# The feed-forward down projection by Strassen's seven block products instead of 22 plain steps, in a one-core fp32 kernel of two transformer blocks

## The chip, the core and the metric

One core of a Trainium2 chip runs the whole program as one launch. The metric is the device time of that core in microseconds (us), taken over several runs; lower is better. The profile is of one execution.

## The reference

Two transformer blocks on a batch of one with 1024 tokens of width 1024, all in fp32: retention and pooling mixers, cross attention, a feed-forward layer, then a gated delta rule layer ("GDN") and a forgetting attention. The change touches only the last matrix product of the feed-forward layer of the first block. `D_FF` is 2816.

```python
def conv_glu_ffn(h, w_up, conv_w, conv_b, w_down):
    a = h @ w_up
    ...
    c = conv_w[0] * a2 + conv_w[1] * a1 + conv_w[2] * a + conv_b
    gate, val = jnp.split(c, 2, axis=-1)
    return (jax.nn.silu(gate) * val) @ w_down
...
        x = x + conv_glu_ffn(rmsnorm(x, ffn_norm_g[l]), ffn_w_up[l], ffn_conv_w[l],
                             ffn_conv_b[l], ffn_w_down[l])
    return rmsnorm(x, final_norm_g)
```

## The kernel before

Everything is kept transposed: a tile has 128 channels on the partitions and tokens along its length. Each fp32 operand is split into a high part, rounded to the matmul format (ScalarE or GpSimd makes it), and a low part, value minus high part (VectorE or GpSimd). One product of a 128 by 128 weight block with 128 by 512 activations is `dot3`: three matmuls of 128x512 (high by high, high by low, low by high, L1011 to L1013) into one half of a PSUM bank pair.

**Around the stage.** The up projection runs in 22 pairs (`PAIRS`), each already by seven block products (`PRODUCTS`), and leaves the gated activation of a pair, 128x1024, in DRAM (`act_store`, L686, from the buffer `taps`). After the last pair VectorE still folds the products together (L3028 to L3053), applies the taps of the convolution (L3062) and the gate (L3073, which counts `ff_prod`). After the down projection comes the final norm, whose sums run beside the first GDN gemm: `next_high` (L2290) and `lo_gained` (L3118) split the rows of x that are finished.

**The down projection.** 22 steps (`DOWN`), eleven for the first four of the eight 128-row tiles of the output and eleven for the last four. In a step TensorE multiplies the eight weight blocks of one 128x1024 slab with two 128x1024 activation tiles: 16 `dot3`, 48 matmuls, into four bank pairs (`DOWN_BANKS`). So 352 `dot3` in all, the plain count for 22 contraction tiles, 8 row tiles and 2 token halves.

**Who feeds it.** SP loads one 512 KB slab of weights a step (`down_load`, L670) and two activation tiles (`ring_load`, L681) into a ring of five buffers; GpSimd splits the slab (`split_slot`, L819 high and L828 low, 128x1024 each); ScalarE makes the high part of the activations (`ring_high_part`, L2238), VectorE the low part (`ring_low`, L3080). The activation tiles are loaded twice but for the last two, 20 times two tiles. At the end of each half VectorE adds the four bank pairs to x in SBUF (`down_add`, L3114, eight of 128x1024). Order on each engine is the program's own, written out by hand: an instruction waits with all that stands behind it. On VectorE `ring_low(0)` stands inside the last pair's work, ahead of L3033, and `ring_low(1)` behind L3053. On SP the eight loads that bring x back (L730) go between the slabs.

## Time and profile before

| | us |
|---|---|
| median of 3 runs | 2753.74 |
| lowest and highest | 2750.53, 2755.33 |
| span of the profiled execution | 2752.7 |
| TensorE busy | 2696.4 (98%) |
| VectorE, ScalarE, GpSimd busy | 1451.5, 1068.8, 1127.4 |
| down projection, first matmul to the first one of the GDN layer | 1117.32 to 1363.83 |

The profile puts a time of start and a duration to each instruction of the four engines and to each DMA. A row of a timeline may join several equal instructions in a row ("x6"); its duration is then from the first one's start to the last one's end. A matmul's record, 0.39 to 0.40 us, overlaps the next one's: the distance of the starts is what counts. Idle time in front of an instruction stands in brackets, with what ended it. The mean granted clock of TensorE in the stage is 1.00.

### The profile page before, as it was taken

Reading aid. Unit: us, or ns where it says so; the run is one execution under the profiler, and the core shown is the slowest. Engines: PE = TensorE matmul, PEld = TensorE weight load, DVE = VectorE, ACT = ScalarE, POOL = GpSimd, SP = SyncE. Lnnn points to the kernel's source line nnn. Section 1 sums busy time; section 2 is a strip of 40 time slices with the busy share of each in tenths; the row PEclk is TensorE's granted clock in tenths of the full one; section 3 lists DMA queues with packets and bytes.
Section 4 is the critical chain, followed back from the end, with each engine's and each line's share of the span. In section 5 each row is a group of like instructions: output and inputs, shape, how many; then the busy total and the mean of one; then the engine's idle time right before and its main releaser. Section 6 shows DMA issues by size and latency. Waiting matters only on the chain.

```text
span 2752.7 us, 34759 instructions
## 1 busy us (share of the span) xinstructions
PE 2696.4 (98%) x13662; PEld 2197.4 (80%) x13662; DVE 1451.5 (53%) x2038; ACT 1068.8 (39%) x1614; POOL 1127.4 (41%) x625
## 2 busy tenths in 40 slices
PE   8999999999999999999999999999998999999998
PEld 6888788777788888788878888888876888888886
DVE  7344643136666666522356666666535455555565
ACT  5322222234444444222244554544534433333342
POOL 4333443224777776433322122222345333333335
PEclk9999999999999999999999999999998999999999
DMA  4112231003222222554322222222222111111114
GB/s 152 31 40 75 101 106 54 25 30 114 71 77 84 77 84 77 192 174 139 122 74 68 67 72 65 70 65 66 65 100 85 39 39 39 39 39 39 39 54 164
DMA packets 111787, 214.24 MB, mean 78 GB/s; under 512 B 32032, under 2 KB 61888, under 8 KB 111504
## 3 DMA queue, kind: packets, MB, share of 16 engines
q1 hardware_dynamic: 104992, 190.02, 21.2%
q10 hardware_dynamic: 6192, 20.18, 2.0%
q8 instruction: 109, 1.79, 0.3%
q0 software_dynamic: 448, 1.88, 0.2%
q14 instruction: 46, 0.38, 0.0%
HBM read 177.38 MB, written 34.67 MB: 77 GB/s over the span
## 4 chain that ended last, share of the span: by engine, by line
PE 88%; DVE 5%; ACT 2%; issue 2%; DMA 1%; POOL 1%; SPq 0%; ACTq 0%; DVEq 0%; POOLq 0%
PE gemm L1011 21%; PE gemm L1012 20%; PE gemm L1013 20%; PE small L1193 2%; PE small L1736 2%; PE small L1013 2%; PE small L1012 2%; PE small L1011 2%; PE small L1724 1%; PE small L1581 1%; PE gemm L1134 1%; PE small L1306 1%; PE small L1326 1%; PE gemm L1137 1%; PE gemm L1138 1%
## 5 line engine op out<-in xcount | busy, mean ns | idle before, releaser
L1011 PE MATMUL gemm<-h_hi,w_hi 128*128 128x512 f32 x2136 | 894.6, 419 | 22.7 <-DVE h_lo L2722 8.9
L1012 PE MATMUL gemm<-h_lo,w_hi 128*128 128x512 f32 x2136 | 845.1, 396 | 0.0
L1013 PE MATMUL gemm<-h_hi,w_lo 128*128 128x512 f32 x1960 | 776.6, 396 | 0.0
L819 POOL TENSOR_TENSOR w_hi<-w_raw,unit_col 128x1024 fp32r<-128x1024 f32 x134 | 262.6, 1960 | 1134.4 <-PE gemm L1013 891.6
L1011 PEld LDWEIGHTS gemm<-h_hi,w_hi 128*128 128x128 f32 x2136 | 403.9, 189 | 106.5 <-issue 11.2
L1012 PEld LDWEIGHTS gemm<-h_lo,w_hi 128*128 128x128 f32 x2136 | 404.3, 189 | 74.8 <-issue 2.9
L1013 PEld LDWEIGHTS gemm<-h_hi,w_lo 128*128 128x128 f32 x1960 | 369.3, 188 | 89.6
L828 POOL TENSOR_TENSOR w_lo<-w_raw,w_hi 128x1024 fp32r<-128x1024 f32 x118 | 305.3, 2587 | 13.8 <-DVE w_lo L2881 4.9
L972 POOL TENSOR_TENSOR w_hi<-w_raw,unit_col 128x1024 fp32r<-128x1024 f32 x32 | 60.8, 1899 | 310.9 <-PE gemm L1013 310.9
L3080 DVE TENSOR_TENSOR t_lo<-t_lo_f,t_hi 128x1024 fp32r<-128x1024 f32 x36 | 44.5, 1282 | 143.1 <-ACT t_hi L2238 143.1
L2541 ACT ACTIVATE xres<-xres,stat 128x128 f32<-128x128 f32 (+3 forms) x64 | 49.7, 777 | 151.0 <-DVE stat L3553 150.7
L3062 DVE SCALAR_TENSOR_TENSOR small<-norm,vec,small 128x1024 f32<-128x1024 f32 x84 | 106.0, 1285 | 1.5
L3547 DVE SCALAR_TENSOR_TENSOR xres<-small,rstd_cols,xres 128x128 f32<-128x128 f32 x64 | 22.4, 350 | 155.9 <-PE small L1013 155.4
L1011 PE MATMUL gemm<-t_hi,w_hi 128*128 128x512 f32 x248 | 98.2, 396 | 0.0
L1012 PE MATMUL gemm<-t_lo,w_hi 128*128 128x512 f32 x248 | 98.1, 396 | 0.0
L2238 ACT ACTIVATE t_hi<-t_lo_f 128x1024 fp32r<-128x1024 f32 x36 | 35.9, 1050 | 156.7 <-DMA t_lo_f<-act_spill 156.7
L2635 ACT ACTIVATE xres<-small 128x512 f32<-128x512 f32 (+2 forms) x96 | 47.1, 491 | 105.5 <-PE small L1724 104.9
L1013 PE MATMUL gemm<-t_hi,w_lo 128*128 128x512 f32 x204 | 80.6, 395 | 0.0
L1736 PEld LDWEIGHTS small<-xres 128*128 128x128 f32 x576 | 74.1, 191 | 5.7
L974 POOL TENSOR_TENSOR w_lo<-w_raw,w_hi 128x1024 fp32r<-128x1024 f32 x32 | 76.8, 2399 | 2.5
L1736 PE MATMUL small<-xres 128*128 128x128 f32 x576 | 74.5, 274 | 0.0
L964 POOL TENSOR_TENSOR w_raw<-w_raw,vec 128x1024 f32<-128x1024 f32 x32 | 66.5, 2078 | 1.8 <-DMA w_raw<-w_stream 1.8
(550 smaller groups left out, 5258.1 us busy)
## 6 DMA issues: line engine op xcount, KB each, us to landing
w_raw<-w_stream SPq DMA_DIRECT2D x178, 512.0 KB, 3.5
t_lo_f<-act_spill SPq DMA_DIRECT2D x36, 512.0 KB, 4.4
act_spill<-taps SPq DMA_DIRECT2D x22, 512.0 KB, 2.9
x_spill<-xres ACTq DMA_DIRECT2D x16, 512.0 KB, 2.7
v_gate<-w_stream SPq DMA_DIRECT2D x11, 512.0 KB, 4.2
v_val<-w_stream SPq DMA_DIRECT2D x11, 512.0 KB, 3.4
xres<-x_t SPq DMA_DIRECT2D x8, 512.0 KB, 8.7
xres<-x_t ACTq DMA_DIRECT2D x8, 512.0 KB, 4.9
```

The costliest lines, as they stand in the source:

```text
L819: nc.gpsimd.tensor_tensor(whi[d][:, :, :], raw[s][:, :, :], unit, ALU.mult).then_inc(w_hi_done, 1)
L828: nc.gpsimd.tensor_tensor(wlo[d][:, :, :], raw[s][:, :, :], whi[d][:, :, :].bitcast(F32), ALU.subtract).then_inc(w_split, 1)
L964: nc.gpsimd.tensor_tensor(raw[s][:, :, :], raw[s][:, :, :], gain.broadcast_to([P, KT, P]), ALU.mult).then_inc(w_gained, 1)
L972: nc.gpsimd.tensor_tensor(whi[s][:, :, :], raw[s][:, :, :], unit, ALU.mult).then_inc(w_hi_done, 1)
L974: nc.gpsimd.tensor_tensor(wlo[s][:, :, :], raw[s][:, :, :], whi[s][:, :, :].bitcast(F32), ALU.subtract).then_inc(w_split, 1)
L1011: mm(dst, w_hi, a_hi, start=first, stop=False, skip_group_check=onto)
L1012: mm(dst, w_hi, a_lo, start=False, stop=False, skip_group_check=onto)
L1013: return mm(dst, w_lo, a_hi, start=False, stop=last, skip_group_check=onto)
L1193: last = nc.tensor.transpose(ck(dst, n), ck(src, n), ident)
L1736: last = mm(ck(pb, 4 + q % 4), ck(X4(0), b), ck(X4(5), b), start=(b == 0), stop=(b == q))
L2541: A(sc, sc, ACT.Exp, bias=stat[:, 14 + z:15 + z], accum_out=stat[:, 15 + z:16 + z]).then_inc(fx_exp, 1)
L3062: ins = V.scalar_tensor_tensor(c, Nf[:, v * FP + n:v * FP + n + S], vc("ff_w", 2 * PAIRS * n + q), c, ALU.mult, ALU.add)
```

## The change

The contraction (22 tiles) is cut in two halves of eleven, the output rows in two halves of four tiles and the tokens in two halves of 512: a 2 by 2 by 2 block product, computed as Strassen's seven. Each product is eleven **units** (one contraction tile each) of four `dot3`, 308 in all, from sums or differences of weight blocks and of activation blocks. They run in four groups: two products beside each other, three times (`part` 0 in `A_BANKS`, `part` 1 in `B_BANKS`, the latter one unit behind), then one product alone. n counts units over the groups, so unit 11 is the first of group 1 (the groups are numbered 0 to 3). The operations of one unit, all 128x512 or 128x4x128:

| group | GpSimd: sums L1136, low L1153 | ScalarE highs | VectorE: sums L3364, lows L3369, L3375, late L3380, L3385 | `dot3` |
|---|---|---|---|---|
| 0 | 1, 1 | 4 | 4 | 8 |
| 1 | 2, 1 | 4 | 5 | 8 |
| 2 | 1, 1 | 4, 5 from u = 3 | 4 (u = 0, 1), 5 (u = 2), 6 from u = 3 | 8 |
| 3 | 1, 0 | 1 | 1, and `lo_gained` | 4 |

The split weights and the split sums lie in buffers three deep: what is prepared for unit n waits until unit n - 3 has been multiplied (`unit_mm` at n - 2). "Late" operations prepare in group 2, from u = 2, the activation sums of group 3. In a unit of groups 0 to 2 the order on GpSimd is sum(s), wait for ScalarE's high part, low. When a product ends, its four banks of 128x512 are added to one or two of the four quarters of x: 48 additions (L3401) of 128x512; the next group may not write a bank until they are done.

Activations stay in SBUF as halves of tokens (`B11`, `B21`, `B12`, `B22`, eleven strips each, in the buffers of `h_hi_f`, `h_lo_f`, `yt` and `head`) and are loaded once, up to five strips a DMA (`act_load`, L840). Weight slabs are loaded 52 times (`raw_load`, L835) into six buffers, then four others. On SP slabs 4 and 5 of that list stand behind the last `act_store`.

```diff
-DOWN = [(0, i) for i in range(FF_STEPS)] + [(1, FF_STEPS - 1), (1, FF_STEPS - 2)] + [(1, i) for i in range(FF_STEPS - 2)]
...
+SLABS = (((0, 1), (1, 1)), ((0, 0), (1, 1), (0, 1)), ((0, 0), (1, 0)), ((1, 0), (1, 1)))
+N_RAW, N_LATE = 6, 4
...
+        TARGETS = {(0, 0): ((C21, ALU.add), (C22, ALU.subtract)), (0, 1): ((C11, ALU.add), (C21, ALU.add)),
+                   (1, 0): ((C11, ALU.add), (C22, ALU.add)), (1, 1): ((C22, ALU.add),),
+                   (2, 0): ((C12, ALU.add), (C22, ALU.add)), (2, 1): ((C11, ALU.subtract), (C12, ALU.add)),
+                   (3, 0): ((C11, ALU.add),)}
...
+        A_BANKS = [b[:, c * HALF:(c + 1) * HALF] for b in (ps[0], gp[1]) for c in range(2)]
+        B_BANKS = [b[:, c * HALF:(c + 1) * HALF] for b in (ps[1], gp[0]) for c in range(2)]
...
+            act_load(R2, (0, 4), (SECOND[0], 0), b21_in[0])
+            raw_load(3)
             act_store(PAIRS - 1)
...
+            act_load(R2, (4, 8), (SECOND[4], 0), b21_in[1])
+            for j in (4, 5, 6, 7):
+                raw_load(j)
...
+                if g == 0:
+                    down_sum(n, (0, 1), (1, 1), (0, 1), ALU.add)
+                elif g == 1:
+                    down_sum(n, (0, 0), (1, 1), (1, 1), ALU.add)
+                    down_sum(n, (0, 1), (0, 0), (0, 1), ALU.subtract)
...
+                pool.wait_ge(*w_rounded(2 * n + 1))
+                nc.gpsimd.tensor_tensor(dw_low(n, 0), dw_value(n, 0), dw_hi(n, 0).bitcast(F32), ALU.subtract).then_inc(w_a_ready.sem, 1)
...
+            for g in range(GROUPS):
+                for u in range(UNITS):
+                    unit_products(UNITS * g + u, 0)
+                    if u and g < GROUPS - 1:
+                        unit_products(UNITS * g + u - 1, 1)
+                if g < GROUPS - 1:
+                    unit_products(UNITS * g + UNITS - 1, 1)
...
                 if p == PAIRS - 1:
-                    ring_low(0)
+                    down_t_low(0, 0)
...
                 if p == PAIRS - 1:
-                    ring_low(1)
+                    down_w_low(0)
+                    down_t_low(1, 0)
+                    down_t_sum(0, 1)
+                    down_w_low(1)
+                    down_t_low(0, 1)
                 tap(p, 0, 1)
                 tap(p, 0, 0)
+                if p == PAIRS - 1:
+                    down_t_sum(1, 1)
+                    down_w_low(2)
+                    down_t_low(2, 0)
                 tap(p, 1, 1)
+                if p == PAIRS - 1:
+                    down_t_low(1, 1)
                 tap(p, 1, 0)
                 product(p)
...
+                for part in range(2):
+                    if g and u == part:
+                        for q in range(4):
+                            bank_add(g - 1, part, q)
```

**The end of the up projection.** On VectorE, in the kernel before, from the last pair's work with gemm1 to the gate (lines as in the profile):

```order
L3080 TENSOR_TENSOR h_lo<-h_lo_f,h_hi 128x1024 x2
L3033 TENSOR_TENSOR tiny<-gemm1,tiny 128x512
L3035 TENSOR_TENSOR gemm1<-gemm1,poolw 128x512
L3041 TENSOR_TENSOR gemm0<-gemm0,tiny 128x512
L3043 TENSOR_TENSOR norm<-gemm0,norm 128x512
L3049 TENSOR_TENSOR gemm1<-gemm1,tiny 128x512
L3051 TENSOR_TENSOR gemm1<-gemm1,tiny 128x512
L3053 TENSOR_TENSOR norm<-gemm1,norm 128x1024
L3080 TENSOR_TENSOR h_lo<-h_lo_f,h_hi 128x1024 x2
L3062 SCALAR_TENSOR_TENSOR taps<-norm,vec,taps 128x1024 x4
L3073 TENSOR_TENSOR taps<-taps 128x1024
```

The same place in the changed kernel, first the head and then what stands from its L3322 (L3053 before) to the gate:

```order
L3369 TENSOR_TENSOR h_lo<-h_hi_f,h_lo 128x512
L3302 TENSOR_TENSOR tiny<-gemm1,tiny 128x512
```

```order
L3322 TENSOR_TENSOR norm<-gemm1,norm 128x1024
L3375 TENSOR_TENSOR w_lo1<-w_raw1,w_lo1 128x512
L3369 TENSOR_TENSOR h_lo<-h_hi_f,h_lo 128x512
L3364 TENSOR_TENSOR h_lo_f<-yt,h_hi_f 128x512
L3375 TENSOR_TENSOR w_hi1<-w_raw1,w_hi1 128x512
L3369 TENSOR_TENSOR h_lo<-h_lo_f,h_lo 128x512
L3331 SCALAR_TENSOR_TENSOR taps<-norm,vec,taps 128x1024 x2
L3364 TENSOR_TENSOR h_lo_f<-yt,h_hi_f 128x512
L3375 TENSOR_TENSOR norm_r<-tiny,norm_r 128x512
L3369 TENSOR_TENSOR h_lo<-h_hi_f,h_lo 128x512
L3331 SCALAR_TENSOR_TENSOR taps<-norm,vec,taps 128x1024
L3369 TENSOR_TENSOR h_lo<-h_lo_f,h_lo 128x512
```

Two operations of 128x1024 ahead of L3033 have become one of 128x512; the two ahead of the taps have become nine of 128x512, spread between them.

**Group 1.** On GpSimd, the operations of unit 11; in the kernel before a step had the two of the second fence:

```order
L1136 TENSOR_TENSOR w_raw0<-norm,w_raw0 128x4x128
L1136 TENSOR_TENSOR w_raw1<-w_raw1,norm 128x4x128
L1153 TENSOR_TENSOR w_ex<-w_raw0,w_ex 128x512
```

```order
L819 TENSOR_TENSOR w_hi<-w_raw,unit_col 128x1024
L828 TENSOR_TENSOR w_lo<-w_raw,w_hi 128x1024
```

On VectorE, one unit in the midst of group 1, where the kernel before had two operations of 128x1024 a step:

```order
L3364 TENSOR_TENSOR h_lo_f<-h_hi_f,head 128x512
L3364 TENSOR_TENSOR h_lo_f<-h_hi_f,h_lo_f 128x512
L3369 TENSOR_TENSOR h_lo<-h_lo_f,h_lo 128x512 x2
L3375 TENSOR_TENSOR w_hi1<-w_raw1,w_hi1 128x512
```

None of the five has an operand in PSUM. The additions out of the banks stand between two units; here those of group 1's first product, at the start of group 2:

```order
L3375 TENSOR_TENSOR w_hi1<-norm,w_hi1 128x512
L3401 TENSOR_TENSOR xres<-xres,small0 128x512 x4
L3401 TENSOR_TENSOR xres<-xres,gemm1 128x512 x4
L3364 TENSOR_TENSOR h_lo_f<-h_hi_f,yt 128x512
L3369 TENSOR_TENSOR h_lo<-h_lo_f,h_lo 128x512
L3369 TENSOR_TENSOR h_lo<-yt,h_lo 128x512
L3375 TENSOR_TENSOR norm_r<-norm,norm_r 128x512
```

Eight additions of 128x512 stand ahead of all activation sums and lows of the next unit. The same stage end in the kernel before had one addition of 128x1024 for each bank pair and nothing to prepare behind it but a step that was due later.

## Rows read from the trace of the kernel before

**Rows 1.** The page: span; busy time of the engines; the chain by engine.

```profile
span 2752.7 us, 34759 instructions
...
PE 2696.4 (98%) x13662; PEld 2197.4 (80%) x13662; DVE 1451.5 (53%) x2038; ACT 1068.8 (39%) x1614; POOL 1127.4 (41%) x625
...
PE 88%; DVE 5%; ACT 2%; issue 2%; DMA 1%; POOL 1%; SPq 0%; ACTq 0%; DVEq 0%; POOLq 0%
```

**Rows 2.** Busy time by stretch: the down projection.

```profile
core 0: us, PE busy (x) PEld busy (x) DVE busy (x) ACT busy (x) POOL busy (x), PEclk, DMA share, GB/s
1117.20:1363.80 246.60, 246.60 (x1058) 197.98 (x1057) 76.16 (x62) 51.38 (x51) 95.03 (x44) 1.00 0.44 152
```

**Rows 3.** Timeline of PE: the last product of the up projection, and both ends.

```profile
start us, us, engine line op out<-in xcount [idle before <-releaser]
1112.34 0.40 PE L1013 MATMUL gemm<-t_hi,sum_ex_r 128*128 128x512 f32 x1
1114.47 0.47 PE L1011 MATMUL gemm<-t_hi,pair_ex 128*128 128x512 f32 x1 [1.74 <-DVE tiny L3033]
...
1117.32 0.39 PE L1011 MATMUL gemm<-h_hi,w_hi 128*128 128x512 f32 x1
```

```profile
1363.83 0.39 PE L1011 MATMUL gemm<-h_hi,w_hi 128*128 128x512 f32 x1
```

**Rows 4.** Timeline of DVE across the start of the stage.

```profile
1109.67 4.06 DVE L3080 TENSOR_TENSOR h_lo<-h_lo_f,h_hi 128x1024 fp32r<-128x1024 f32 x2 [4.25 <-ACT h_hi L2238]
1113.65 0.68 DVE L3033 TENSOR_TENSOR tiny<-gemm,tiny 128x512 f32<-128x512 f32 x1
...
1117.52 0.70 DVE L3049 TENSOR_TENSOR gemm<-gemm,tiny 128x512 f32<-128x512 f32 x1 [0.49 <-PE gemm L1013]
1118.12 0.69 DVE L3051 TENSOR_TENSOR gemm<-gemm,tiny 128x512 f32<-128x512 f32 x1
1118.85 1.23 DVE L3053 TENSOR_TENSOR norm<-gemm,norm 128x1024 f32<-128x1024 f32 x1
1119.99 2.54 DVE L3080 TENSOR_TENSOR h_lo<-h_lo_f,h_hi 128x1024 fp32r<-128x1024 f32 x2
...
1127.60 1.22 DVE L3073 TENSOR_TENSOR taps<-taps 128x1024 f32<-128x1024 f32 x1
```

**Rows 5.** The line L2967, VectorE, min/median/max ns; and DVE at its last four.

```profile
L2967 DVE TENSOR_TENSOR t_lo<-t_lo_f,t_hi x12: 681/684/1775, 644.5 to 692.5; 128x512 fp32r<-128x512 f32 x12
```

```profile
688.48 5.75 DVE L2967 TENSOR_TENSOR t_lo<-t_lo_f,t_hi 128x512 fp32r<-128x512 f32 x4
```

**Rows 6.** Timeline of POOL: one alone, and three beside those four.

```profile
661.91 1.30 POOL L927 TENSOR_TENSOR w_raw<-w_raw 128x512 f32<-128x512 f32 x1
...
690.39 1.61 POOL L927 TENSOR_TENSOR v_val<-v_val 128x512 f32<-128x512 f32 x1
692.08 1.60 POOL L936 TENSOR_TENSOR sum_ex<-v_val,v_gate 128x512 f32<-128x512 f32 x1
693.75 1.62 POOL L908 TENSOR_TENSOR v_gate_r<-v_gate,w_hi 128x512 fp32r<-128x512 f32 x1
```

**Rows 7.** Timelines of DVE and POOL at the end: an operand in PSUM, and none.

```profile
1364.03 1.22 DVE L3114 TENSOR_TENSOR xres<-small,xres 128x1024 f32<-128x1024 f32 x1 [0.39 <-PE small L1013]
1365.17 1.88 DVE L3118 SCALAR_TENSOR_TENSOR h_lo<-xres,both_g,h_hi 128x1024 fp32r<-128x1024 f32 x1
```

```profile
1364.07 1.90 POOL L819 TENSOR_TENSOR w_hi<-w_raw,unit_col 128x1024 fp32r<-128x1024 f32 x1 [6.74 <-PE small L1013]
```

**Rows 8.** Timeline of ACT: a high part of 128x512.

```profile
1084.79 0.63 ACT L2125 ACTIVATE w_hi<-v_gate 128x512 fp32r<-128x512 f32 x1 [1.25 <-PE gemm L1013]
```

**Rows 9.** Landing time of a slab (page), and two stretches with their DMA rate.

```profile
w_raw<-w_stream SPq DMA_DIRECT2D x178, 512.0 KB, 3.5
```

```profile
1100.00:1120.00 20.00, 18.26 (x79) 14.33 (x77) 14.45 (x15) 7.43 (x9) 9.83 (x4) 1.00 0.77 254
1120.00:1124.00 4.00, 4.00 (x19) 3.14 (x18) 3.96 (x5) 1.24 (x1) 0.31 (x1) 1.00 1.02 401
```

More of the change, by code:

```diff
@@ new lines, in build, with raw_view @@
+        W_TWO = ((whi[0][:, :, :], wlo[1][:, :, :]), (wlo[0][:, :, :], whi[1][:, :, :]), (w_ex[:, :, :], tile8(N_r[:, 3, :])))
+        W_LATE = [tile8(hlo[:, k, :]) for k in (4, 5, 6)]
+        RAWS = [raw[0][:, :, :], raw[1][:, :, :], tile8(const[:, CONST_AT["dmat"]:CONST_AT["dmat"] + S]),
+                tile8(tiny[:, :, :].rearrange("p i x -> p (i x)")),
+                tile8(N[:, 0, :]), tile8(N[:, 1, :])] + [tile8(hhi_f[:, k, :]) for k in range(4, KT)]
+        def raw_view(n, half, row):
+            return RAWS[raw_of(raw_for(n, half, row))].rearrange("p (q k) m -> p k q m", k=2)[:, odd_of(n, half)]
@@ new lines, in dt_low, with dt_value, summed @@
+        def dt_low(n, part):
+            return T_LO[n % 3][part] if n < N_TWO else B21_r[n % UNITS]
+        def dt_value(n, part):
+            g, u = divmod(n, UNITS)
+            if (g, part) == (0, 0):
+                return B11[u]
+            if (g, part) == (2, 1):
+                return B22[u]
+            return T_SUM[n % 3][part]
+        def summed(g, part):
+            return (g, part) not in ((0, 0), (2, 1))
+        C11, C12, C21, C22 = (KT // 2, 0), (KT // 2, 1), (0, 0), (0, 1)
@@ new lines, in t_sums, with w_sums, bank_count @@
+        def t_sums(n, part):
+            return sum(summed(m // UNITS, at) for m, at in ORDER[:t_place(n, part)])
+        def w_sums(n, part):
+            g, u = divmod(n, UNITS)
+            return sum(W_SUMS[:g]) * UNITS + W_SUMS[g] * u + (1 + part if g == 1 else 1)
+        def bank_count(g, part, q):
+            done = 0
+            for key in TARGETS:
+                each = 1 if key == (2, 0) else len(TARGETS[key])
+                if key == (g, part):
+                    return done + each * (q + 1)
+                done += 4 * each
@@ new lines, in _ @@
+            act_load(R2, (10, 11), (SECOND[10], 0), b21_in[1])
+            for k in range(KT):
+                if k == KT // 2:
+                    for j in (8, 9):
+                        raw_load(j)
+                sp.dma_start(xres[:, k, :], x_keep[k]).then_inc(x_back.sem, 16)
+            raw_load(10)
+            act_load(R2, (UNITS, 2 * KT), (SECOND[0], 1), b22_in)
+            act_load(R1, (UNITS, 2 * KT), (FIRST[0], 1), b12_in)
+            for j in (11, 12, 13):
+                raw_load(j)
@@ L733, in g_row @@
+            act_load(R2_H, (0, 5), (SECOND[CUT], 1), b22_in)
+            act_load(R2_H, (5, 6), (SECOND[UNITS - 1], 1), b22_in)
+            act_load(R1_lo, (0, UNITS - CUT), (FIRST[CUT], 1), b12_in)
+            for j in range(14, len(RAW_LOADS)):
+                raw_load(j)
             def g_row(h):
@@ L2277, in _ @@
                     high_a22(p + 1)
+            down_t_high(0, 1)
             tap2(PAIRS - 1, 1)
+            down_w_high(2, 0)
+            down_t_high(2, 0)
+            down_w_high(2, 1)
+            down_t_high(1, 1)
             gate(PAIRS - 1)
-            for j in range(2, FF_STEPS + 1):
-                ring_high_part(j)
+            for n in range(3, N_TWO):
+                g, u = divmod(n, UNITS)
+                if u == 0:
+                    down_t_high(n - 1, 1)
+                down_w_high(n, 0)
+                down_t_high(n, 0)
+                down_w_high(n, 1)
+                if u:
+                    down_t_high(n - 1, 1)
+                if g == GROUPS - 2 and u >= 3:
+                    down_late_high(u - 3)
+            down_t_high(N_TWO - 1, 1)
+            for u in range(UNITS - 3, UNITS):
+                down_late_high(u)
             def next_high(k):
```

444 lines of the change are left out of this document (312 added, 132 removed).

## The prediction, made before the run

> **What bounds the kernel now.** I read the page first: TensorE is busy 98% of the span and makes 88% of the chain that ends last [rows 1]. Then the table by stretches for the down projection: 246.6 us, TensorE busy for all of them at a granted clock of 1.00, while VectorE works 76, ScalarE 51 and GpSimd 95 us there, and the DMA moves 152 GB/s [rows 2]. So in this stage TensorE is the bound, the others have room, and work taken from it is worth its full time until another engine is full. From the first matmul to the first of the next layer [rows 3] it is 1363.83 - 1117.32 = 246.51 us for 352 `dot3`: 0.70 us each. All other questions are whether VectorE, GpSimd, ScalarE and the DMA can feed a TensorE that needs less.
>
> **TensorE's own gain.** 308 `dot3` in place of 352: 44 x 0.70 = **-30.8 us**. It all lies on the path.
>
> **The last pair of the up projection.** TensorE stalls 1.74 us for L3033, which waited on VectorE behind two ring lows that took 4.06 us [rows 3, 4]. Now one operation of 128x512 stands there, at most 1.78 us [rows 5], so L3033 is done early enough that TensorE goes on at 1112.34 + 0.23 = 1112.57 in place of 1114.47: **-1.9 us**, and the stage may start at 1115.4.
>
> **What one operation costs on VectorE and GpSimd.** This is the step the rest hangs on. A VectorE operation of 128x512 takes 0.68 us alone and starts 0.60 after the last one [rows 4, 5], and one of GpSimd 1.30 [rows 6]. But the slowest of L2967's twelve took 1.775 us, and four in a row took 5.75 us, just where GpSimd's operations went from 1.30 to 1.61 each and started 1.69 apart [rows 5, 6]: the two engines take turns, one operation of each in 1.69 us. VectorE loses 1.69 - 0.60 = 1.09 us at each such meeting. It is not so where VectorE reads PSUM: L3114 kept its 1.22 us under a GpSimd operation that covers it, while L3118 right after it, with no PSUM operand, took 1.88 [rows 7]. All preparation of the new stage is without PSUM operands; the 48 additions have one and cost 0.60 each, undisturbed. I take GpSimd's 128x4x128 sums at the 1.30 of 128x512, as the nearest row with two plain operands; bounds are 1.27, no gain from the form, and 1.6, the value under contention.
>
> The Trainium skill (SBUF — State Buffer, section "SBUF: two separate sides") calls this port an exclusive lock: whoever starts first keeps it for the whole instruction and the other fully blocks. By it a meeting would cost VectorE the full 1.30, 0.21 more than the rows' 1.09, and the sum would be larger by 0.21 x (3 x 11 + 2 x 8) = 10 us. The rows decide for turns of 1.69. The same section confines the lock to VectorE operations with two SBUF inputs; by that rule, the trace agrees for L3114.
>
> **Start of the stage: +9.4 us.** If TensorE never waited, unit 4 would start after seven blocks of 4 x 0.70 = 2.8 us: 1115.4 + 19.6 = 1135.0. Its weights are slabs 4 and 5, which SP issues only once `ff_prod` is complete. That was 1127.60 + 1.22 = 1128.8 [rows 4]. Now: 1.9 earlier; less 2.5 for the ring lows that went; plus nine operations of 0.60, 5.4; plus two or three meetings of 1.09, for units 1 to 3 are being prepared on GpSimd meanwhile, 2.5: about 1132.4. Behind it SP issues 0.5 MB of the store, 1 MB of activations and then the two slabs, 1 MB. At some 400 GB/s [rows 9] 2.6 MB take 6.6 us, and a lone slab of 0.5 MB takes 3.5, 2.2 more than its 1.3 of transfer [rows 9]: landed at 1141. Then sum 1.3, high 0.63 [rows 8], low 1.3: TensorE at 1144.4. Smaller waits before it (the bank of L3322 at 1118.1, the lows of units 1, 2 and 3 behind taps) are inside these 9.4. Bounds: 7.4, with no meeting before `ff_prod`; 12, with all transfers at 254 GB/s [rows 9] and partly hidden.
>
> **Group 0, otherwise: 0.** Four VectorE and two GpSimd operations a unit: 2 x 1.69 + 2 x 0.60 = 4.6 us, against 8 x 0.70 = 5.6 of TensorE, which hides them. ScalarE's four take 2.5.
>
> **Group 1: +15.5 us.** Five VectorE operations and three meetings: 5 x 0.60 + 3 x 1.09 = 6.27, and 0.24 for handing over between the engines: 6.51 us a unit. TensorE's 5.6 no longer cover it: 0.91 x 11 = 10.0. At the boundary the 16 additions of group 0 (9.6 us) stand ahead of the next units' sums; buffers three deep give back some of it; 5.5 stay. Bounds: 3.3, all of it the boundary, with no meetings; 19, with GpSimd at 1.6 for the sums.
>
> **Group 2: +17.0 us.** From u = 3 on six VectorE operations, two meetings, and a gap of 1.3 us while the two late operations and the lows wait for ScalarE in order: 3.6 + 2.2 + 1.3 = 7.1 us against 5.6: 1.5 x 8 = 12.0, with 0.8 before; boundary with 12 additions (group 1's) 4.2. Bounds: 6, if VectorE fills its gaps (2 x 1.69 + 4 x 0.60 = 5.8 a unit); 19.
>
> **Into group 3: +4.1 us.** Unit 33's weights need ScalarE and VectorE behind the last late lows, and its banks the eight additions of the product before: some four us between 4 and 6. Inside group 3 a unit needs one operation of each engine in 2.8 us: nothing.
>
> **End: +1.5 us.** Three `lo_gained` now come together with the last four additions, and the chain of the final norm that followed L3118 starts later by a bit more than one operation of 1.2 us. Bounds 0 and 3.
>
> **Sum.** -30.8 - 1.9 + 9.4 + 15.5 + 17.0 + 4.1 + 1.5 = +14.8 us. The profiled execution's span is 2752.7, 1.0 below the median of the runs, so 2767.5 of span, **2768 us** of time: TensorE gives up 31 us of work and gets 46 of waiting.
>
> **Rival A: TensorE stays the bound (faster).** If sums and lows of VectorE and GpSimd meet seldom, because GpSimd runs ahead of VectorE by a unit and they fall in each other's gaps, VectorE needs 3.6 us a unit at most and group 1 waits 3.3, group 2 0.9, the start 7.4, the last boundary 4.2: 15.8. Then -32.7 + 15.8 + 1.5 = -15.4: 2738 us. For it: stages in which both engines are half busy and TensorE runs on. Against: in group 1 GpSimd works 3.9 of 5.6 us, and rows 5 and 6 show every operation met. It decides from a cost of a meeting under 0.5 us: then group 1 needs 3.0 + 1.5 + 0.2 = 4.7.
>
> **Rival B: the meetings are there but fall into idle time (no change).** VectorE's loop is then its bare capacity: group 1 6.27, so 0.67 x 11 = 7.4 and 3.3 at the boundary; group 2 5.8, so 1.4 and 4.2; start 9.4; last boundary 4.1: 29.8. Net -1.4: 2752 us. For it: the gap of 1.3 in group 2 is worked out from an order of waits that no row shows. Against: in-order waits rarely close up by themselves.
>
> **Rival C: the DMA (slower still).** Between 1134 and 1180 some 18 MB must come (slabs 6 to 14, x, the rest of the activations), 393 GB/s. The stretch of 1120 to 1124 gave 401, the 20 us around it 254 [rows 9]. At 254 it is 71 us in place of 46; 5.5 of the 25 would hide in group 1's boundary: +19.5, 2788 us. The Trainium skill (DMA: Bandwidth & Descriptors, section "Specifications") names 358 GB/s as a core's share of HBM; by that estimate it would be 50 us, and +4; the trace shows 401, above it.
>
> **Rival D: the change does not do what it says.** The count of matmuls is in the instruction order, 924 for 1056; nothing there could fail unseen. No chance of its own.
>
> **Chances.** Forecast 0.60 (2756 to 2779, from the bounds of its terms: start -2 to +2.6, group 1 -6 to +3.5, group 2 -8 to +2, taken as not all going one way); rival A 0.12; rival B 0.17; rival C 0.11. The range that holds 8 in 10 takes in the forecast's and B's and most of C's: 2749 to 2789. A measurement of this kernel tells 0.2%, 5.5 us, from no change. Faster by more: A and a bit of B, 0.13. Within: the most of B and the forecast's lowest edge, 0.17. Slower: 0.70.
>
> **What would show it.** In the profile of the changed kernel: TensorE's unit in group 1 every 6.5 us, with idle ended by VectorE's t_low or w_low (L3369, L3375) and these at 1.7 us where GpSimd's L1136 and L1153 run; a unit in group 2 every 7.1; unit 4 released by GpSimd behind a slab that landed near 1141; TensorE's first GDN matmul 13 us after 1363.8. Rival A shows units of 5.6 us; B 6.3 and 5.8; C idle ended by L1136 behind a DMA in group 0 or at unit 11. I am wrong if meetings are rare, or if the late operations of group 2 do not hold the sums of the next unit.

## The result and the profile after

| | before | after |
|---|---|---|
| median of 4 runs each, us | 2754.53 | 2779.45 |
| lowest, highest | 2750.53, 2758.9 | 2778.07, 2781.06 |
| span of the profiled execution | 2752.7 | 2777.4 |
| start of the down projection | 1117.32 | 1114.37 |
| first matmul of the next layer | 1363.83 | 1379.58 |

The ratio is 1.0087, with a 95% interval of 1.0073 to 1.0101: slower, by 24.9 us. TensorE has 30.8 us less to do and the program takes 25 us longer.

The page of the changed kernel, its span, busy times and chain by engine, as [rows 1] of before:

```profile
span 2777.4 us, 35061 instructions
...
PE 2682.0 (97%) x13530; PEld 2178.7 (78%) x13530; DVE 1602.0 (58%) x2214; ACT 1114.0 (40%) x1728; POOL 1161.5 (42%) x669
...
PE 82%; DVE 9%; issue 3%; ACT 3%; DMA 2%; POOL 1%; SPq 0%; ACTq 0%; DVEq 0%; POOLq 0%
```

The chain of waits now goes through VectorE for 9% of the span where it was 5% [rows 1]. Busy time by stretch (columns as in [rows 2]): the whole stage, the 10 us before the last gate, and the 6 us behind the longest stall.

```profile
1114.30:1379.60 265.30, 227.46 (x926) 173.87 (x926) 225.56 (x238) 95.79 (x162) 132.82 (x88) 0.97 0.42 154
1145.00:1151.00 6.00, 3.92 (x9) 3.15 (x10) 5.41 (x5) 3.33 (x8) 5.15 (x4) 0.50 1.04 408
1123.00:1133.00 10.00, 6.57 (x24) 4.96 (x23) 9.96 (x8) 4.51 (x8) 4.43 (x3) 0.83 0.00 1
```

In [rows 2] TensorE was busy for all of 246.6 us and VectorE for 76; here TensorE stands still for 38 of 265 and VectorE is busy for 226. The mean granted clock of the stage is 0.97, and in the second stretch 0.50, that is 1.2 GHz: this the prediction had in no term. TensorE's busy time falls by 14 us and not by 31, in part because a matmul at half clock counts as busy for longer.

The difference of the two traces, place by place. "Idle" is the distance of two starts less 0.233 us, summed over the gaps of a place (a place's units are those that the prediction's term counted); "half clock" is what matmuls 0.43 us apart cost over 0.233.

| place | forecast | measured |
|---|---|---|
| program before the last pair (unchanged) | 0 | -1.0 |
| last pair of the up projection | -1.9 | -2.0 |
| 308 products for 352 | -30.8 | -30.9 |
| start of the stage, to unit 5 | +9.4 | +11.6 idle, +3.3 half clock |
| group 1 | +15.5 | +11.6 |
| group 2, with its last unit | +17.0 | +15.5 idle, +1.5 half clock |
| into and in group 3 | +4.1 | +4.8 |
| small gaps | 0 | +1.4 |
| end: from the first product of the next layer to its small gates | +1.5 | +8.1 |
| behind it | 0 | +0.8 |
| sum | +14.8 | +24.7 |

### The profile page after: what moved, and what is told of

It reads as the page before. It is cut to its first block, busy times and chain, and to the rows that moved or that the text cites. A ratio compares the mean times of both kernels' runs of the same rounds, so it can differ in the third digit from the quotient of the medians.

```text
span 2777.4 us, 35061 instructions
## 1 busy us (share of the span) xinstructions
PE 2682.0 (97%) x13530; PEld 2178.7 (78%) x13530; DVE 1602.0 (58%) x2214; ACT 1114.0 (40%) x1728; POOL 1161.5 (42%) x669
## 3 DMA queue, kind: packets, MB, share of 16 engines
q8 instruction: 108, 1.77, 0.3%
q0 software_dynamic: 448, 1.88, 0.2%
## 4 chain that ended last, share of the span: by engine, by line
PE 82%; DVE 9%; issue 3%; ACT 3%; DMA 2%; POOL 1%; SPq 0%; ACTq 0%; DVEq 0%; POOLq 0%
PE gemm L1213 20%; PE gemm L1214 19%; PE gemm L1215 19%; PE small L1953 2%; PE small L1395 2%; PE small L1941 1%; DVE h_lo_f L3364 1%; PE small L1796 1%; PE gemm L1336 1%; PE gemm L1339 1%; PE gemm L1340 1%; PE small L1508 1%; PE small L1528 1%; PE small L1213 1%; DVE xres L3401 1%
## 5 line engine op out<-in xcount | busy, mean ns | idle before, releaser
L1214 PE MATMUL gemm<-h_lo,w_hi 128*128 128x512 f32 x2164 | 857.0, 396 | 0.0
L996 POOL TENSOR_TENSOR w_hi<-w_raw,unit_col 128x1024 fp32r<-128x1024 f32 x112 | 220.0, 1965 | 983.9 <-PE gemm L1215 885.4
L1005 POOL TENSOR_TENSOR w_lo<-w_raw,w_hi 128x1024 fp32r<-128x1024 f32 x96 | 250.0, 2604 | 12.1 <-DVE w_lo L3150 4.9
L1174 POOL TENSOR_TENSOR w_hi<-w_raw,unit_col 128x1024 fp32r<-128x1024 f32 x32 | 60.6, 1895 | 311.2 <-PE gemm L1215 311.2
L1953 PEld LDWEIGHTS small<-xres 128*128 128x128 f32 x576 | 74.1, 191 | 5.6
L1176 POOL TENSOR_TENSOR w_lo<-w_raw,w_hi 128x1024 fp32r<-128x1024 f32 x32 | 76.8, 2399 | 2.5
L3202 DVE TENSOR_REDUCE stat<-small 128x4 f32<-128x1024 f32 x8 | 9.8, 1225 | 106.2 <-PE small L1508 106.2
L3302 DVE TENSOR_TENSOR tiny<-gemm,tiny 128x512 f32<-128x512 f32 x22 | 15.2, 691 | 91.8 <-PE gemm L1215 91.8
L2718 ACT ACTIVATE v_new<-small,gdn_cols 128x128 f32<-128x128 f32 x64 | 23.5, 367 | 108.6 <-PE small L1721 108.6
L2441 ACT ACTIVATE small<-norm,vec 128x1024 f32<-128x1024 f32 x42 | 50.8, 1210 | 36.4 <-DVE norm L3312 20.5
L2481 ACT ACTIVATE h_lo<-h_lo_f 128x512 fp32r<-128x512 f32 x37 | 23.3, 629 | 101.8 <-DVE h_lo_f L3364 101.8
```

The costliest lines, as they stand in the source:

```text
L996: nc.gpsimd.tensor_tensor(whi[d][:, :, :], raw[s][:, :, :], unit, ALU.mult).then_inc(w_hi_done, 1)
L1005: nc.gpsimd.tensor_tensor(wlo[d][:, :, :], raw[s][:, :, :], whi[d][:, :, :].bitcast(F32), ALU.subtract).then_inc(w_split, 1)
L1174: nc.gpsimd.tensor_tensor(whi[s][:, :, :], raw[s][:, :, :], unit, ALU.mult).then_inc(w_hi_done, 1)
L1176: nc.gpsimd.tensor_tensor(wlo[s][:, :, :], raw[s][:, :, :], whi[s][:, :, :].bitcast(F32), ALU.subtract).then_inc(w_split, 1)
L1214: mm(dst, w_hi, a_lo, start=False, stop=False, skip_group_check=onto)
L1953: last = mm(ck(pb, 4 + q % 4), ck(X4(0), b), ck(X4(5), b), start=(b == 0), stop=(b == q))
```

## The experiments

Single executions on other chips differ by a few microseconds, so the experiments are compared by the stage's length (first matmul of the down projection to the first of the next layer; 265.2 us after, 246.5 before) and by what lies in it; a ratio is given where several rounds were run. The two runs of experiment 5 that leave the stage as it is have 263.1 and 263.6 us, so a difference of 2 us in a single execution says nothing. "Group" is the time from a group's first matmul to the next group's.

**1. Do VectorE and GpSimd take turns?** The midst of group 1 in the changed kernel, TensorE, VectorE and GpSimd:

```profile
1218.26 0.47 PE L1213 MATMUL small<-h_lo,w_hi 128*128 128x512 f32 x1 [0.71 <-DVE h_lo L3369]
1224.76 0.47 PE L1213 MATMUL small<-h_lo,w_lo 128*128 128x512 f32 x1 [0.75 <-DVE h_lo L3369]
1231.28 0.47 PE L1213 MATMUL small<-h_lo,w_ex 128*128 128x512 f32 x1 [0.70 <-DVE h_lo L3369]
```

```profile
1225.31 1.80 DVE L3375 TENSOR_TENSOR w_hi<-w_raw,w_hi 128x512 fp32r<-128x512 f32 x1
1227.04 1.77 DVE L3364 TENSOR_TENSOR h_lo_f<-h_hi_f,head 128x512 f32<-128x512 f32 x1
1228.74 1.79 DVE L3364 TENSOR_TENSOR h_lo_f<-h_hi_f,h_lo_f 128x512 f32<-128x512 f32 x1
1230.45 1.47 DVE L3369 TENSOR_TENSOR h_lo<-h_lo_f,h_lo 128x512 fp32r<-128x512 f32 x2
```

```profile
1225.27 1.30 POOL L1153 TENSOR_TENSOR w_ex<-tiny,w_ex 128x512 fp32r<-128x512 f32 x1 [1.81 <-ACT w_ex L2466]
1226.53 1.74 POOL L1136 TENSOR_TENSOR tiny<-const,tiny 128x512 f32<-128x512 f32 x1
1228.23 1.75 POOL L1136 TENSOR_TENSOR norm<-norm,const 128x512 f32<-128x512 f32 x1
```

A unit takes 6.50 and 6.52 us, released by VectorE's low. Of five VectorE operations the three that stand beside one of GpSimd's take 1.77 to 1.80, the other two 0.7 each; VectorE waits 0.1 us in a unit. That is the prediction's loop; the two runs that follow ask whether GpSimd is its cause.

The first takes one meeting away. It leaves out the second of GpSimd's two sums, and the group's second product takes the unsummed blocks:

```diff
                 elif g == 1:
-                    down_sum(n, (0, 0), (1, 1), (1, 1), ALU.add)
-                    down_sum(n, (0, 1), (0, 0), (0, 1), ALU.subtract)
+                    nc.gpsimd.tensor_tensor(raw_view(n, 1, 1), raw_view(n, 0, 0), raw_view(n, 1, 1), ALU.add).then_inc(w_summed.sem, 2)
```

> The changed kernel, with the second of the two weight sums that GpSimd makes in a unit of group 1 left out (the second product of that group takes the unsummed blocks; no other wait or transfer changes). Theory (VectorE and GpSimd take turns; each meeting costs VectorE 1.09 us): VectorE's five operations meet two instead of three, 5 x 0.60 + 2 x 1.09 + 0.24 = 5.4 us, under TensorE's 5.53, so a unit in the midst of group 1 falls from 6.5 to 5.5 us and group 1 loses about 7 us of waiting. Rival (VectorE is held by its own five operations and by waits for ScalarE, GpSimd costs nothing): a unit stays at 6.5 us.

Group 1 fell from 74.1 to 66.7 us, its idle time from 11.6 to 4.3, all of the rest at its boundary. Between 1217 and 1250 TensorE does not wait at all. VectorE's own operations are the same, and it hardly waited for ScalarE before or after (0.1 us a unit), so the rival falls.

The second adds two meetings where there was no wait:

```diff
                 if g == 0:
                     down_sum(n, (0, 1), (1, 1), (0, 1), ALU.add)
+                    if n >= 5:
+                        pool.wait_ge(*w_a_ready(n))
+                        for i in range(2):
+                            nc.gpsimd.tensor_tensor(tile8(N[:, 2, :])[:, 4 * i:4 * i + 4, :], raw_view(n, 1, 1), raw_view(n, 1, 1), ALU.add)
```

> The changed kernel, with two GpSimd additions of 128x512 more in each unit of group 0 from the sixth on; they write into a row that nobody reads, and stand in front of GpSimd's wait for ScalarE. Theory (turns): VectorE's four operations all meet one, 4 x 1.69 = 6.8 us, so these units go from 5.53 to 6.8 to 7.0 us, some 7 us more in all. Rival (GpSimd costs nothing by itself): its four operations take 5.2 us alone, less than 5.53, and the units stay.

VectorE and TensorE in that run:

```profile
1168.28 1.52 DVE L3379 TENSOR_TENSOR w_hi<-w_raw,w_hi 128x512 fp32r<-128x512 f32 x1
1169.72 1.52 DVE L3368 TENSOR_TENSOR h_lo_f<-yt,h_hi_f 128x512 f32<-128x512 f32 x1
1171.17 1.78 DVE L3373 TENSOR_TENSOR h_lo<-h_hi_f,h_lo 128x512 fp32r<-128x512 f32 x1
1172.87 1.77 DVE L3373 TENSOR_TENSOR h_lo<-h_lo_f,h_lo 128x512 fp32r<-128x512 f32 x1
```

```profile
1173.09 0.47 PE L1217 MATMUL small<-h_lo,w_ex 128*128 128x512 f32 x1 [0.16 <-DVE h_lo L3373]
1179.39 0.47 PE L1217 MATMUL small<-h_lo,w_hi 128*128 128x512 f32 x1 [0.51 <-DVE h_lo L3373]
1185.67 0.48 PE L1217 MATMUL small<-h_lo,w_lo 128*128 128x512 f32 x1 [0.53 <-DVE h_lo L3373]
```

All four VectorE operations are long now, and two units go from 5.53 to 6.30 and 6.28 us (of the six with added operations the first two stayed at 5.5, the third took 5.9 and the last 5.7); group 0 went from 76.3 to 80.7. The direction is as the theory says, the size below its 6.8: the two added operations read one operand twice, and a meeting with such a one takes 1.45 us (1168.28 to 1169.72), not 1.70, so that a unit of two such meetings and two full ones is 6.3 us.

**2. All of it to VectorE.** If GpSimd's help costs VectorE 1.1 us an operation and doing it itself costs 0.60, VectorE should do it alone. The edit moves sums and the first low from GpSimd's loop into VectorE's from the third unit on, and places the late operations as in the first edit of experiment 3 ("the run before" in its expectation):

```diff
+            def down_w_sum(n, i=0):
...
+                V.tensor_tensor(raw_view(n, *left), raw_view(n, *left), raw_view(n, *right), op).then_inc(w_summed.sem, 1)
...
             for n in range(3, N_TWO):
+                down_w_sum(n)
                 down_t_sum(n, 0)
+                if g == 1:
+                    down_w_sum(n, 1)
                 down_t_sum(n - 1, 1)
...
+                down_w_low_a(n)
                 down_t_low(n, 0)
                 down_w_low(n)
```

> The changed kernel, with GpSimd's work of the stage from the third unit on (weight sums and the first weight low, two or three operations a unit, one in group 3) given to VectorE, and the late operations placed as in the run before. GpSimd is then idle in the stage. Theory (turns): VectorE has eight operations a unit at 0.60 = 4.8 us with nobody to meet, under TensorE's 5.53: units of groups 1 and 2 at 5.5 us, only the boundaries and the start remain; about 2762 us against 2779. Rival (VectorE is full by its count of operations; a unit of group 1 shows 1.3 us an operation): eight would take 10 us a unit, 2860 us or more.

The same 45 us of group 1, first the changed kernel and then this run (columns as in [rows 2]):

```profile
1210.00:1255.00 45.00, 39.72 (x166) 30.35 (x165) 44.24 (x37) 16.66 (x30) 29.15 (x20) 1.00 0.30 109
```

```profile
1210.00:1255.00 45.00, 45.00 (x196) 36.56 (x195) 40.62 (x67) 19.68 (x33) 0.00 (x0) 1.00 0.41 152
```

VectorE does 67 instructions in less busy time (40.6 us) than 37 before (44.2), and TensorE never stops. 2768.95 us, ratio to the kernel before 1.0048 (1.0030 to 1.0065). The seven microseconds that were missing to 2762 have their own causes: units of group 2 took 6.57 us and not 5.5, with a wait of VectorE for ScalarE of 1.66 us in each (next experiment), and group 3, where VectorE's sums now stood in order behind slabs that landed late (waits of 1.4 to 5.2 us for them), went from 33.1 to 44.5 us.

**3. The late operations of group 2.** In the changed kernel VectorE and ScalarE there:

```profile
1296.84 0.69 DVE L3369 TENSOR_TENSOR h_lo<-h_lo_f,h_lo 128x512 fp32r<-128x512 f32 x1 [0.70 <-ACT h_lo L2481]
1297.88 0.69 DVE L3369 TENSOR_TENSOR head_r<-yt,head_r 128x512 fp32r<-128x512 f32 x1 [0.35 <-ACT head_r L2481]
```

```profile
1303.21 0.63 ACT L2481 ACTIVATE h_lo<-h_lo_f 128x512 fp32r<-128x512 f32 x1 [4.32 <-DVE h_lo_f L3364]
```

VectorE waits 1.05 us a unit for a ScalarE that has itself stood idle for 4.3: the sum, the high and the low of one operand stand too close together. The first edit put the late sum and low between them:

```diff
+                if g == GROUPS - 2 and u >= 2:
+                    down_late_sum(u - 2)
+                if g == GROUPS - 2 and u >= 3:
+                    down_late_low(u - 3)
                 down_t_low(n, 0)
...
                 down_w_low(n)
-                if g == GROUPS - 2 and u >= 2:
-                    down_late_sum(u - 2)
-                if g == GROUPS - 2 and u >= 3:
-                    down_late_low(u - 3)
```

> The changed kernel, with VectorE's late sum and late low of group 2 put between the activation sum and the first low of the unit, in place of behind the weight low. Same operations. Theory: 1.05 us of each unit of group 2 are waits of VectorE for ScalarE (0.70 before the first low, 0.35 before the second); the two late operations fill them, a unit falls from 7.04 to about 6.0 us, and group 2 by 7 to 9 us. Rival (the capacity of the pair VectorE and GpSimd is used up): a unit stays at 7.0.

The stage stayed at 264.0 us and group 2 at 79.3 (81.7 in the changed kernel, 80.1 in the two runs that leave it as it is). Single units ran unevenly, between 5.5 and 9.1 us; the seven from the third on took 6.9 on average. The expected gain did not come, yet this is not the rival's verdict, for the idle time was still there, elsewhere. VectorE in that run:

```profile
1298.96 0.69 DVE L3385 TENSOR_TENSOR yt_r<-yt,yt_r 128x512 fp32r<-128x512 f32 x1 [1.66 <-ACT yt_r L2486]
```

The late low waits for its high, and ScalarE works that off last, behind the high of the very sum that VectorE has just made. The second edit also moves it on ScalarE:

```diff
+                if g == GROUPS - 2 and u >= 3:
+                    down_late_high(u - 3)
                 down_w_high(n, 0)
...
-                if g == GROUPS - 2 and u >= 3:
-                    down_late_high(u - 3)
```

> As the run with the late operations between sum and lows, and ScalarE's late high put in front of the other highs of its unit, so that VectorE's late low finds it ready. Theory (in that run VectorE waited 1.66 us for ScalarE, in order behind the high of the unit's sum): no waits are left, 6 x 0.60 + 2 x 1.09 + 0.2 = 6.0 us a unit in group 2 against 7.04, 8 us less in all. Rival (capacity): 7.0 stays.

A unit takes 5.82 us, group 2 72.2 in place of 81.7 and the stage 255.9. Between 1290 and 1320 VectorE does not wait at all there: its six operations with their meetings fill the 5.8 us, and the other 1.2 us a unit of the changed kernel were an order.

**4. The start.** SP's slabs 4 and 5 landed at 1143.1; the row of GpSimd behind them, and TensorE's behind that:

```profile
1143.11 1.26 POOL L1136 TENSOR_TENSOR norm<-norm 128x512 f32<-128x512 f32 x1 [14.19 <-DMA norm<-w_stream]
```

```profile
1127.87 0.76 PE L1213 MATMUL small<-h_lo,w_ex 128*128 128x512 f32 x1 [3.43 <-DVE h_lo L3369]
...
1147.08 0.77 PE L1213 MATMUL small<-h_lo,w_lo 128*128 128x512 f32 x1 [6.41 <-DVE h_lo L3369]
1147.64 0.63 PE L1214 MATMUL small<-h_lo,w_lo 128*128 128x512 f32 x1
1148.07 0.63 PE L1215 MATMUL small<-h_lo,w_lo 128*128 128x512 f32 x1
```

The DMA had been idle from 1123 to 1133 (share 0.00 in the table above): everything stood behind the gate. The edit gives the two slabs another place, two rows of x that are free by then, and moves SP's issues ahead of the store:

```diff
+        XROWS = [tile8(xres[:, k, :]) for k in (1, 2)]
...
                 elif j in (4, 5):
-                    sp.wait_ge(ff_prod, PAIRS)
+                    sp.wait_ge(*prod_mm(PRODUCTS * PAIRS))
...
+            act_load(R2, (4, 8), (SECOND[4], 0), b11_in[0])
+            for j in (4, 5):
+                raw_load(j)
             raw_load(3)
             act_store(PAIRS - 1)
-            act_load(R2, (4, 8), (SECOND[4], 0), b21_in[1])
```

> The changed kernel, with the first use of slabs 4 and 5 moved from two rows of norm, which the taps still read, to two rows of x that are free once the last product of the up projection is done; SP issues them, and strips 4 to 7 of B21, ahead of the store of the last gated activation, and VectorE waits for those strips alone. Theory (the long stall before unit 4 is the way from the gate over the store to those slabs): the stall of 6.6 us before unit 4 falls to about 1, and since TensorE no longer stands still that long, its nine matmuls at half clock behind the stall (2.0 us) go too: 6 to 8 us less. Rival (VectorE's taps, gate and preparation alone hold unit 4): the stall shrinks by less than 3 us.

There is no gap before unit 4 any more; the stage is 258.2 us, 7.0 less, with 4.1 us idle left before unit 2, whose low stands on VectorE behind two taps and a wait of 1.2 us for ScalarE.

**5. The end, and the clock.** The prediction gave 1.5 us to the end; the trace shows 8.1. VectorE's three splits of x, met by GpSimd's first weight splits, and TensorE behind them:

```profile
1380.39 5.98 DVE L3434 SCALAR_TENSOR_TENSOR h_lo<-xres,both_g,h_hi 128x1024 fp32r<-128x1024 f32 x3
...
1381.77 3.40 DVE L3434 SCALAR_TENSOR_TENSOR h_lo<-xres,both_g,h_hi 128x1024 fp32r<-128x1024 f32 x1
...
1386.29 0.68 DVE L3485 COPY head<-small 128x512 f32<-128x512 f32 x1
```

```profile
1380.85 3.23 POOL L1005 TENSOR_TENSOR w_lo<-w_raw,w_hi 128x1024 fp32r<-128x1024 f32 x1
```

```profile
1397.66 6.99 PE L1686 MATMUL small<-const,head 128*128 128x1 f32 x32 [3.77 <-DVE head L3490]
```

Only the middle split (3.40 us, in the first row as one of the three) was held up for long; the others took 1.46 and 1.27. With them VectorE's chain for the norm starts 6.7 us after the first product of the next layer, where it started 3.1 after it before: that is TensorE's 3.6 us of new idle time. The other 4.5 of the 8.1 lie behind it: from the first of the 32 narrow matmuls to the small gates it is 14.1 us here and 9.6 before. The narrow ones took 3.73 us in the kernel before and 6.99 here, and 12 products behind them ran 0.43 us apart. Before, seven products did so too, at a granted clock of 0.50 with no more than 0.2 us idle in front of the narrow matmuls (columns as in [rows 2]):

```profile
1382.60:1385.60 3.00, 3.00 (x9) 2.32 (x8) 0.72 (x5) 0.30 (x1) 0.00 (x0) 0.50 0.51 144
```

The first run fills TensorE's idle time and changes nothing else:

```diff
                 if s == 9:
+                    pe.wait_ge(down_ev, KT)
+                    for _ in range(16):
+                        mm(gp[1][:, half(0)], whi[0][:, 0, :], hhi[:, 0, half(0)], start=True, stop=True)
                     pe.wait_ge(sq_added, SQ_FIN + 2 * KT)
```

> The changed kernel, with 16 matmuls of 128x512 more, into a bank whose contents have been added and that the next tile overwrites, in the 3.8 us in which TensorE stands still before L1686 at the end of the stage. Theory (part of the loss at the end is TensorE's clock, which falls after the idle time): with the gap filled L1686's 32 narrow matmuls take 3.7 us as before the change, not 7.0, and the products behind them run at 0.233 and not 0.43 us apart: 4 to 5 us less from the last addition to the small gates' product. Rival (the slow stretch has another cause, VectorE or the weights): no gain, or the cost of the filler.

```profile
1392.01 3.90 PE L1685 MATMUL gemm<-h_hi,w_hi 128*128 128x512 f32 x16
1395.87 5.09 PE L1689 MATMUL small<-const,head 128*128 128x1 f32 x32
```

L1686 (L1689 there) took 5.09 us, and the way from L1686 to the small gates 11.2 in place of 14.1: 2.9 us less, though VectorE was not touched. In five other runs with this end unchanged the same way took 12.6 to 13.8 and the narrow matmuls 6.5 to 7.0, so 1.4 to 2.9 us are what the stall costs through the clock. The expected 3.7 was not reached: from the twentieth on the narrow matmuls were slow even behind busy time.

The second run removes the cause, the order on VectorE:

```diff
-            for k in range(KT // 2, KT - 1):
-                lo_gained(k)
+            lo_gained(KT // 2)
             for i in range(2 * (KT - SUM_PE)):
...
-                if i == 3:
-                    lo_gained(KT - 1)
+            for k in range(KT // 2 + 1, KT):
+                lo_gained(k)
+            dve.wait_ge(h_lo_done, KT * HGDN + KT)
```

> The changed kernel, with only the first of the last three splits of x (lo_gained) ahead of the sums of the final norm on VectorE, and the others behind them. Theory (TensorE waits before L1686 for VectorE's sums, which stand behind three splits of 2.0 us each): the sums start 3 to 4 us earlier, the idle time before L1686 goes, and with it part of the slow clock behind it: 5 to 7 us less from the first product of the next layer to the small gates' product. Rival (ScalarE's squares hold the sums): under 2 us.

```profile
1392.03 3.63 PE L1686 MATMUL small<-const,head 128*128 128x1 f32 x32
```

No idle time, 3.63 us, and 22.1 us from the first product of the next layer to its small gates, where the changed kernel has 32.2 and the kernel before 24.1: 10 us less, more than the 5 to 7 expected. Not all of it is the order's: TensorE's clock stayed at 1.00 through this end, where the kernel before had its stretch at 0.50. Two later runs with the same order took 23.6 us, 8.6 less.

**6. Do the losses add up?** The three repairs of order of 3, 4 and 5 together, GpSimd kept at its work:

> The changed kernel with the three repairs of order that were run one by one (slabs 4 and 5 in rows of x; late operations between sum and lows with ScalarE's late high first; one split of x ahead of the norm's sums), and GpSimd kept at its work. Theory (the losses are separate places and add up): 2779.4 - 8 - 12 - 8 = 2752 us, no measurable difference from the kernel before, and group 1 still at 6.5 us a unit, 11 to 12 us idle. Rival (they share a cause, so that one repair gives what another gave): 2758 or more.

2758.12 us against 2758.97 for the kernel before on the same chip, ratio 0.9999 (0.9989 to 1.0008). The stage is 252.0 us, group 1 still has 11.4 us idle, and the end is 23.6. So stage and end together are 22 us shorter, where the three repairs gave 26 one by one: 13.2 of 16.3 in the stage, 8.6 of 10.1 at the end. The losses are separate places, and they add up but for some 4 us, part of it half clock that now shows at the start of group 3. What remains over the bare 215.6 us of products eats Strassen's 31 us: about 8 at the start, 12 in group 1 (6.2 of them waits beyond the boundary, from meetings), 9 in group 2 and 6 in group 3.

**7. A version that beats both.** All of it together, VectorE in place of GpSimd, two more buffers for group 3's slabs, and the last two taps and the gate put off to units 3 to 5:

> The changed kernel with what the theory asks for, together: GpSimd's work from the third unit on given to VectorE; ScalarE's late high first; slabs 4 and 5 in rows of x; two more buffers for the slabs of group 3; the last two taps and the gate of the up projection put between units 3 to 6; at the end only one of the three splits of x ahead of the norm's sums. Theory: starts about 3 us idle, group 1 only its boundary (5 + 3 at half clock), group 2 4 us, group 3 3 us, end 2 us: 2740 us, faster than the kernel before. Rival (VectorE with eight operations a unit and 48 additions has no room for the boundaries): 2755 or more.

2750.64 us, ratio 0.9973 (0.9960 to 0.9986), not the 2740 expected: the gate had become late, the store and all that SP has behind it with it. Two stretches of its table by stretches:

```profile
1124.00:1142.00 18.00, 15.83 (x69) 12.55 (x68) 16.94 (x26) 9.73 (x17) 0.00 (x0) 1.00 0.04 15
1150.00:1187.00 37.00, 29.06 (x123) 22.94 (x122) 18.48 (x30) 10.76 (x20) 0.00 (x0) 0.91 1.01 390
```

18 us with an idle DMA, then 37 full, and TensorE waited 7.7 us at its end. This is the prediction's rival C, which the change itself did not meet. The last run puts the gate right behind unit 3, sorts SP's queue by need and, in group 3, puts the banks' additions ahead of the late operations; of its edit only SP's part is shown:

```diff
+            for j in (6, 7):
+                raw_load(j)
+            x_row(0)
+            x_row(7)
             act_store(PAIRS - 1)
+            for j in (8, 9):
+                raw_load(j)
...
+            raw_load(10)
+            raw_load(11)
             act_load(R2, (UNITS, 2 * KT), (SECOND[0], 1), b22_in)
             act_load(R1, (UNITS, 2 * KT), (FIRST[0], 1), b12_in)
...
+            for k in (5, 6, 1, 2):
+                x_row(k)
```

> The run with everything together, whose profile showed the DMA idle from 1124 to 1143 (the store of the last activation waited for the late gate) and full from 1150 to 1187, and TensorE waiting 7.8 us for it at unit 10. Here the taps and the gate stand right behind unit 3, the slabs of the next units stand ahead of the rows of x in SP's order, two rows of x come before the store, and at the start of group 3 the additions of the banks stand ahead of the late operations that are needed last. Theory: the 7.8 us and the waits at group 1's first units shrink to 3 or 4 together, group 3's 4.7 to 2: 2742 us. Rival (the same bytes in the same time: the DMA is the bound there whatever the order): 2750 as before.

**2737.45 us**, ratio to the kernel before 0.9919 (0.9905 to 0.9933). Its stage, and the DMA's busiest stretch:

```profile
1114.30:1343.70 229.40, 218.31 (x925) 173.05 (x924) 204.52 (x322) 97.98 (x161) 8.89 (x5) 0.99 0.49 181
...
1143.00:1190.00 47.00, 45.76 (x195) 35.81 (x193) 38.51 (x65) 16.24 (x29) 0.00 (x0) 1.00 0.77 293
```

The stage is 229.5 us long, 14 over the bare 215.6 of its products and 17 less than before the change, and the rival (same bytes, same time) falls: the share of the DMA is 0.77. What is left: 3.7 us idle at the start, 4.5 at group 1's boundary, where 16 additions of banks stand in VectorE's order, with 1.5 at half clock behind it, 0.9 in group 2 and 3.6 in group 3. The edit changes several things at once; no run says what each is worth.

## Why the prediction was right, and where it was off

The direction, the mechanism and the range held: 2779 us lies in 2749 to 2789, slower by more than the 0.2%. But the forecast was a shift of 14 us and 25 came. The result lies at the very edge of the band that the forecast gave itself (2756 to 2779); the room above it in the range was there for rival C, which did not happen. So the range held in part by luck.

- **TensorE's own gain and the last pair** came as worked out: -30.9 and -2.0.
- **The cost of a meeting** was the step on which most hung, and it held: 6.51 us were forecast for a unit in group 1 and 6.50 measured, 7.1 in group 2 and 7.03 measured. The agreement to 0.01 us is partly luck: the 0.24 for handing over had no row behind it, and the trace shows 0.1 us of waiting and meetings of 1.70 to 1.73. Experiments 1 and 2 show that it is GpSimd. The "fully blocks" of the Trainium skill (SBUF — State Buffer, section "SBUF: two separate sides") would have given 10 us more by the prediction's estimate; the trace shows operations of GpSimd starting 1.70 apart with one of VectorE between them, as [rows 5, 6] had it. Beside two SBUF inputs that section names a second case of the lock, a VectorE operation in a 2-port performance mode; the prediction left it out, and no run here shows it.
- **Groups 1 and 2 as sums** were 3.9 and 1.5 us too high in idle time. For group 1 I multiplied by 11 and put the boundary on top; but three units lie in the boundary and the last one does not wait, since VectorE prepares group 2 by then, so seven are left (6.4 us for 10.0). Its boundary was 5.2 (5.5 forecast). In group 2 the eight units from u = 3 on have the 12.0 us that were forecast, but not evenly: 9.2 in seven and 2.7 before the last. There GpSimd had run ahead into group 3's four sums, and VectorE met it more than twice:

```profile
1330.64 1.77 DVE L3364 TENSOR_TENSOR h_lo_f<-h_lo_f,head 128x512 f32<-128x512 f32 x1
```

```profile
1328.43 6.80 POOL L1136 TENSOR_TENSOR h_hi_f<-h_hi_f 128x512 f32<-128x512 f32 x4
```

The boundary of group 2 was 2.6 (4.2 forecast), its third unit 0.9 (0.8).

- **The gap of 1.3 us in group 2** was called an inference from an order of waits. It was 1.05 us, and it was an order: experiment 3 removed it. Rival B's 5.8 us a unit is what group 2 reaches once that order is repaired (5.82); in the change as it stands it did not happen.
- **The start** was too low, 14.9 against 9.4. The gate ended at 1133.1 (1132.4 forecast), but the slabs landed at 1143.1, not 1141, and the low of unit 4 stood behind two more hand-overs: idle 11.6, still inside the upper bound of 12. The other 3.3 are half clock, and with them the term is outside the bound, since that had only transfers in it.
- **The clock** was in no term. At the start 3.3, before group 3 1.5, at the end 4.5: some 9 us, nearly all of the 10 that were missing. This is what the sum lacked most. That the other misses come to almost nothing together is luck: idle time at the start 2.2 too low and at the end 2.1, small gaps 1.4, group 3 0.7, groups 1 and 2 5.4 too high. [Rows 2] showed 1.00 for a stage in which TensorE never stops; a forecast with 46 us of stalls should have asked what TensorE runs at behind each.
- **The end** failed outright: 1.5 with bounds of 0 and 3, measured 8.1, of which 3.6 are idle and 4.5 clock. I counted one operation of 1.2 us; three splits stood there, 6.0 us together because GpSimd splits the next layer's weights at the same time, which [rows 7] showed for this very line (1.88), and behind them a chain of 16 operations that TensorE waits for.
- **Group 3** had 4.8 for 4.1, and I had named the low of unit 33 and the additions. What the prediction lacked is how they follow on each other. VectorE and TensorE at that place in the changed kernel:

```profile
1342.65 0.69 DVE L3375 TENSOR_TENSOR h_lo<-h_hi_f,h_lo 128x512 fp32r<-128x512 f32 x1 [3.25 <-ACT h_lo L2466]
1343.26 1.89 DVE L3385 TENSOR_TENSOR yt_r<-yt,head_r 128x512 fp32r<-128x512 f32 x3
1345.07 2.47 DVE L3401 TENSOR_TENSOR xres<-xres,small 128x512 f32<-128x512 f32 x4
```

```profile
1346.49 0.47 PE L1213 MATMUL small<-yt_r,h_lo 128*128 128x512 f32 x1 [2.16 <-DVE xres L3401]
```

The additions, whose banks had long been ready (the product's last matmul started at 1338.0), stand behind a low that waits 3.25 us for ScalarE and behind three late lows that nobody needs for eight units; TensorE then waits for them bank by bank (4.2 us). The other 0.6 us is one wait near the end of the group.
- **Rival C** was rightly held unlikely: between 1134 and 1180 the DMA moved 17.95 MB, the 18 that the prediction counted, at 390 GB/s, and TensorE waited for none of it behind unit 4. **Rival A** fell with the first row of group 1.

## What to carry to other kernels

Before work is given to GpSimd beside a VectorE that has only SBUF operands, price the meeting, not the operation: here GpSimd's help cost VectorE 1.1 us and doing the same itself 0.60. When TensorE's work shrinks below what feeds it, the order of each feeding queue becomes the time: look for an engine that waits while the one it waits for was idle just before. And sum the additions at group boundaries and the chain behind the last group as stages of their own.
